# Six of 31 depthwise taps moved from VectorE to GpSimd, in a transformer block's convolution

## The reference

```python
def second_block(x, ...):
    h = x * (1.0 + scale) + shift
    proj = h @ w_in
    q, k, v, g_attn, glu_a, glu_b, g_conv = split(proj)
    y_attn = banded_sink_attention(q, k, v, rel_bias, sinks) * silu(g_attn)
    y_conv = conformer_conv(glu_a, glu_b, conv_w, conv_b, ...) * silu(g_conv)
    y = concatenate([y_attn, y_conv]) @ w_out
    return layer_norm(ALPHA * x + gate * y, ln_g, ln_b)

def conformer_conv(glu_a, glu_b, conv_w, conv_b, ln_g, ln_b, w_pw, b_pw):
    u = glu_a * sigmoid(glu_b)
    u = depthwise_causal_conv(u, conv_w) + conv_b      # width 31, 1024 channels
    u = silu(layer_norm(u, ln_g, ln_b))
    return u @ w_pw + b_pw
```

## Time and profile before

| what | us |
|---|---|
| runs of the kernel before: median of 3 | 3560.97 |
| lowest, highest | 3556.67, 3564.26 |
| span of the profiled execution | 3557.2 |
| PE busy over the span | 3344.6 (94%) |
| DVE busy over the span | 2211.8 (62%) |
| POOL busy over the span | 235.6 (7%) |
| first tap to the end of the last sum, on DVE | 2721.92 to 3012.60 |

### The profile page before, as it was taken

The page is one execution under the profiler, slowest core; times in us unless marked ns, Lnnn a source line. Parts: engine busy times, 40 slices in busy tenths (PEclk is TensorE's granted clock), DMA queues, the critical chain, the costliest instruction groups (busy, mean ns, idle before and its releaser), DMA issues.

```text
span 3557.2 us, 49004 instructions
## 1 busy us (share of the span) xinstructions
PE 3344.6 (94%) x16744; PEld 2686.2 (76%) x16744; DVE 2211.8 (62%) x3152; ACT 1341.8 (38%) x2047; POOL 235.6 (7%) x435
## 2 busy tenths in 40 slices
PE   5899979999999999998999999999989998998996
PEld 0799978787777777878788777777867776787784
DVE  0676757766676747566656767656556888445433
ACT  0445534333344433236323444443235221444323
POOL 0000000000000000101000001000100000000000
PEclk8899989999999999999999999999999999999998
DMA  9555555553333324645655344323643222221231
GB/s 399 207 213 197 190 197 201 179 211 133 116 116 118 115 78 168 213 157 186 219 182 177 139 139 153 139 93 120 212 144 118 86 91 83 80 80 59 104 118 68
DMA packets 100616, 533.31 MB, mean 150 GB/s; under 512 B 16976, under 2 KB 17008, under 8 KB 57104
## 3 DMA queue, kind: packets, MB, share of 16 engines
q1 hardware_dynamic: 47232, 343.95, 26.7%
q0 software_dynamic: 53264, 187.75, 15.6%
HBM read 509.57 MB, written 22.02 MB: 149 GB/s over the span
## 4 chain that ended last, share of the span: by engine, by line
PE 72%; DVE 11%; issue 6%; DMA 5%; DVEq 3%; ACT 2%; ACTq 1%; POOL 0%; POOLq 0%; SPq 0%
PE acc L1038 21%; PE acc L1040 20%; PE acc L1039 20%; DVE xy L1922 5%; PE pv L1139 2%; DMA xy<-in_wm 2%; PE S L1120 2%; DMA gates<-in_wm 2%; DVE w_lo L1427 2%; DVEq L1921 1%; PE misc L1294 1%; PE S L1128 1%; DVE gates L1471 1%; ACT h_hi L578 1%; PE misc L1059 1%
## 5 line engine op out<-in xcount | busy, mean ns | idle before, releaser
L1038 PE MATMUL acc<-h_hi,w_hi 128*128 128x512 f32 (+1 forms) x4736 | 1753.8, 370 | 92.4 <-DVE h_lo L1433 42.3
L1039 PE MATMUL acc<-h_lo,w_hi 128*128 128x512 f32 (+1 forms) x4736 | 1714.2, 362 | 0.0
L1040 PE MATMUL acc<-h_hi,w_lo 128*128 128x512 f32 (+1 forms) x4736 | 1713.5, 362 | 0.0
L1038 PEld LDWEIGHTS acc<-h_hi,w_hi 128*128 128x128 f32 x4736 | 909.9, 192 | 276.7 <-issue 80.5
L1040 PEld LDWEIGHTS acc<-h_hi,w_lo 128*128 128x128 f32 x4736 | 910.9, 192 | 135.7
L1039 PEld LDWEIGHTS acc<-h_lo,w_hi 128*128 128x128 f32 x4736 | 912.0, 193 | 130.9 <-issue 6.7
L1427 DVE TENSOR_TENSOR w_lo<-raw,w_hi 128x1024 fp32r<-128x1024 f32 x592 | 697.1, 1219 | 240.2 <-ACT w_hi L578 236.8
L578 ACT ACTIVATE w_hi<-raw 128x1024 fp32r<-128x1024 f32 x592 | 591.7, 1051 | 32.9 <-DMA raw<-in_w 23.6
L1471 DVE SCALAR_TENSOR_TENSOR gates<-gates,csil 128x512 f32<-128x512 f32 x600 | 440.2, 750 | 136.7 <-DMA gates<-in_wm 97.1
L578 ACT ACTIVATE ev<-acc 128x512 f32<-128x512 f32 (+1 forms) x210 | 111.0, 533 | 994.7 <-PE acc L1040 925.3
L418 POOL DMA_DIRECT2D gates<-in_wm x256 | 136.2, 532 | 1522.2 <-DVE gates L1471 1300.1
(11 more groups left out here) (204 smaller groups left out, 1928.9 us busy)
## 6 DMA issues: line engine op xcount, KB each, us to landing
raw<-in_w SPq DMA_DIRECT2D x296, 1024.0 KB, 4.9
gates<-in_wm POOLq DMA_DIRECT2D x256, 512.0 KB, 4.4
xy<-in_wm SPq DMA_DIRECT2D x32, 1024.0 KB, 8.6
x_d<-xy POOLq DMA_DIRECT2D x2, 4096.0 KB, 12.6
qb<-x_d POOLq DMA_DIRECT2D x16, 256.0 KB, 3.7
kb<-x_d POOLq DMA_DIRECT2D x16, 256.0 KB, 3.7
out_y<-xy POOLq DMA_DIRECT2D x4, 1024.0 KB, 4.2
bias_d<-bias_row POOLq DMA_DIRECT2D x8, 384.0 KB, 20.6
```

The source lines that it names most:

```text
L1038: mm(o, w_hi[:, w], h_hi[:, x], start=n == 0, stop=False)
L1039: mm(o, w_hi[:, w], h_lo[:, x], start=False, stop=False)
L1040: last = mm(o, w_lo[:, w], h_hi[:, x], start=False, stop=n == len(ks) - 1)
```

## The change

The sums over taps 25 to 30 of each channel tile go from DVE to POOL. POOL waits for the store of `x2`, then for each channel tile for `conv_done` (the same event that lets DVE begin), makes the product of tap 25 into an accumulator of its own, `xy[c]`, and for each of the other five taps a product into `qb` or `kb` by turns, a drain, and a sum into the accumulator. It raises `pool_taps` at the end. DVE keeps taps 0 to 24, in parts of 9, 8 and 8, then waits for `pool_taps` and adds POOL's accumulator to its own, before the sum into `t1`.

```diff
+DVE_TAPS = 25
...
+        pool_taps = sem("pool_taps")
...
             residual("b", "bout", x1_d)
             store("b", x2_d, 48)
+
+            pool.wait_ge(x_st, shown(x_st, 48))
+
+            for c in range(8):
+                o = tile(xy, c, SEQ)
+                pool.wait_ge(conv_done, shown(conv_done, CONV0["glu"] + c + 1))
+                for tap in range(DVE_TAPS, TAPS):
+                    x, w = work[:, tap:tap + SEQ], vec("dw", c * TAPS + tap)
+                    if tap == DVE_TAPS:
+                        nc.gpsimd.tensor_scalar(o, x, w, None, ALU.mult)
+                    else:
+                        m = (qb[:], kb[:, 0:SEQ])[tap % 2]
+                        nc.gpsimd.tensor_scalar(m, x, w, None, ALU.mult)
+                        pool.drain()
+                        last = nc.gpsimd.tensor_tensor(o, o, m, ALU.add)
+                last.then_inc(pool_taps, 1)
 
             pool.wait_ge(bias_st, shown(bias_st, 16 * N_HEADS))
...
-            TAP_PARTS = (range(0, 11), range(11, 21), range(21, TAPS))
+            TAP_PARTS = (range(0, 9), range(9, 17), range(17, DVE_TAPS))
...
                 if part == 2:
+                    dve.drain()
+                    dve.wait_ge(pool_taps, shown(pool_taps, c + 1))
+                    tt(u, u, tile(xy, c, SEQ), ALU.add)
                     dve.drain()
                     tt(t1[:], t1[:], u, ALU.add)
```

## The result

| | median, us | lowest to highest | runs |
|---|---|---|---|
| before | 3558.9 | 3555.41 to 3564.26 | 20 |
| changed | 3565.01 | 3557.71 to 3568.36 | 20 |

The ratio is 1.0016, with a 95% interval of 1.0009 to 1.0022: 6 us slower. The direction is the forecast one, and the time lies in the wide range, but the forecast was 21 us, three and a half times as much, and the time also lies just outside the likeliest case's own range of 3566 to 3608 us. The profiled execution has a span of 3564.3 us, 7.1 us above that of before.

The account below looks back on a forecast made before the run. The prediction took DVE to bound the stage, with PE the floor right behind: POOL's 70 us less 13 us in pauses charged 57 us, less 36 us relief, so 21 us longer, 3582 us, in a range of 3521 to 3608 us.

Parts of the forecast that it names:

- the wide range: Whole kernel: 3521 to 3608 us, reaching to the case where POOL does not hold DVE up (27%).
- the likeliest case: DVE and POOL take full turns at POOL's bounded price: 3582 us, own range 3566 to 3608 us, chance 56%.
- What bounds the stage: Stage with the taps: DVE is unbroken work, PE waits for it; PE's floor is 32.65 us a channel tile.
- The relief of 36 us: DVE: six taps less, net of the added sum, 4.6 us in six loop channel tiles, 4.2 us in two written-out.
- Turns, or side by side: POOL beside DVE: full turns make it 21 us longer (56%); no hold on DVE gives 3526 us (27%).
- Partial turns: Rival, 10%: only POOL's sums or part of each instruction hold DVE up, 64% of the cost lost, within 7 us.
- The place: Early in each channel tile: the next weight tile's `lo` is late; PE's `w_lo` waits grow from 17.4 to over 30 us.
- The charge on DVE, 57 us: DVE in the stage: POOL's 70 us in full turns, less 13 us that fit into DVE's pauses.
- The slow POOL: Rival, 7%: a product or sum on POOL takes 1.5 us or more, 83 us longer, 3644 us.
- the break-even: DVE may lose at most 36 of 57 us, 64% of the loss in full turns, before the change is a loss.
- The bounds: POOL's price per channel tile: 6.7 us at DVE's own speeds to 12.0 us at 1.09 us for all eleven instructions.
- POOL late: DVE's wait for `pool_taps` costs only its issue; being late would need eleven instructions of some 2.5 us each.

Follow-up runs that it names:

- the cost alone: Changed kernel, but DVE makes all 31 taps, waits for POOL's unchanged work and leaves out adding POOL's sums: 3599.27 us, ratio 1.0107.
- sums: All 31 taps on DVE, POOL making 11 two-input additions per channel tile whose values go nowhere, against the kernel before: 3633.56 us, ratio 1.0214.
- products: All 31 taps on DVE, POOL making 11 one-input multiplications per channel tile whose values go nowhere, against the kernel before: 3576.08 us, ratio 1.0047.
- memsets: All 31 taps on DVE, POOL only writing, 11 times per channel tile, reading nothing of SBUF, against the kernel before: 3554.91 us, ratio 0.9990.
- PSUM: Changed kernel with DVE's tap accumulator in a free PSUM bank and six taps still on POOL: 3530.17 us, ratio 0.9917 to the kernel before.
- the one with eight taps: DVE's accumulator in PSUM, with eight taps on POOL in place of six: 3530.28 us, ratio 0.9920 to the kernel before.

## Why the prediction was wrong, by its own steps

- *What bounds the stage*: right. DVE's row is unbroken, and taking work off it alone gives 38 us, down to PE at 32.63 us a channel tile (32.65 forecast).
- *The relief of 36 us*: right. The changed kernel and the cost alone differ by just this relief, 3599.27 - 3565.01 = 34.3 us in the medians and 35.3 us in the stage.
- *Turns, or side by side*: right that POOL holds DVE up, wrong that it does so for its whole time. Taps beside POOL last 0.93 and 1.53 us, those late in the channel tile 0.75 us; with the accumulator moved to PSUM, or with POOL only writing, the hold on the taps is gone. But beside a product of 1.56 us a tap waits 0.18 us. Only part of each instruction holds DVE up, and that is the rival *Partial turns*, which had 10% and named the measured result, within 7 us of now. Its share of the cost, 64% give or take 12%, met too (40.5 of 57 us are 71%), but of a cost that was itself mis-sized, so that match is partly luck.
- *The place*: right. The wait for `w_lo` is in more and earlier pieces. I had expected over 30 us of it; it is 25.2 us.
- *The charge on DVE, 57 us*: this step failed. It was made of six products at 0.54 us and five sums at 1.09 us in each channel tile, charged in full turns less the pauses, 70 - 13 = 57 us, and it measured 40.5 us in the run of the cost alone. Two errors stand in it, and they work against each other. The prices were too low: alone, a product is 1.56 us and a sum 1.28 us, 15.8 us for a channel tile and 126 us in all, above the upper bound of 12.0 us that I had set. And the rule "all of POOL's time but what fits in DVE's pauses" was too strong: with the true prices it would give 126 - 13 - 36 = 77 us slower. What DVE loses is 0.20 us for a product and 0.85 us for a sum, so of 126 us of POOL's time about a third. The slow POOL, a rival at 7%, was true of its speed and not of its effect. That the direction came out as forecast is therefore in part luck: the break-even lay at a loss of 36 us, and two errors of opposite sign left the loss just above it.
- *The bounds*: the row taken for the upper bound was of another kind of instruction (issuing a DMA), and the lower one assumed that an instruction's length is the length for which it holds its partner. Neither end bounded the term that mattered, the hold for one instruction. The same sum with the measured holds is 44 - 36 = 8 us, and 6 were measured.
- *POOL late*: right for six taps, DVE does not wait for `pool_taps`. With nine it does, in channel tile 0.

The Trainium skill's page "SBUF — State Buffer" (Who interferes with whom) had named a pair of instructions that contend: a DVE instruction with two inputs in SBUF against a POOL instruction that reads SBUF, and not against one that only writes. For the taps, five runs agree (the change, sums, products, memsets, PSUM). The same page's statement (Summary: rules for kernel authors) that the second one is blocked until the first finishes does not fit what the engines show: beside a product of 1.56 us a tap waits 0.18 us. The Trainium skill's page "GPSIMD Engine Reference" (Elementwise — side-by-side cycle accounting) gives, as an estimate from its 2.6 cycles an element, 1.11 us for a sum; measured were 1.28 us.

What is not settled: for how long POOL's product and sum really read. The holds are seen only from DVE's side and at one size, 512 columns, and no run tells why a sum, the shorter instruction, holds a tap four times as long as a product. Nor is it shown whether the tap's second input or its output matters in PSUM, since both moved together, why the first product is held with one tensor input, or why the work behind the stage varies by 5 us.

## What to carry to other kernels

Before work goes from DVE to POOL, look at where both read: DVE's taps, with two inputs in SBUF, paid for each POOL instruction that reads SBUF, here 0.95 us for a product and a sum that relieved DVE of 0.92 us, so what was left was the loss of the added sum: about 0.9 us a channel tile in the loop (38.45 us on average against 37.53 us). The same move gains 28.6 us when DVE's accumulator lies in a free bank of PSUM; that kernel is the fastest complete one here (3530 us), level with the one with eight taps. When a partner's operation is not in the trace, bound the hold on the critical engine and not the partner's own time: POOL's time was 126 us where 70 us had been guessed, the hold 40.5 us where 57 us had been.

## What the runs showed of the hardware that was not expected

- On POOL, a product of 128x512 float32 with one number for each partition is 1.56 us and a sum of two such tiles 1.28 us: the operation with fewer inputs is the slower one. A memset of that size is 0.52 us where nothing meets it.
- The hold goes both ways. POOL's product that meets `w_lo` lasts 3.1 to 3.6 us in place of 1.56 us. In the run with PSUM the one of 3.60 us ends at 2835.56 us, 1.36 us behind both halves of `w_lo`:

```profile
2831.27 2.93 DVE L1445 TENSOR_TENSOR w_lo<-raw,w_hi 128x1024 fp32r<-128x1024 f32 x2
```

- A float32 tap with its accumulator in PSUM costs DVE 755 ns against 752 ns in SBUF; the first product, with one SBUF input, goes from 541 to 808 ns, and to 828 ns beside POOL with both ends in SBUF.
